# A hybrid diffusion backbone step: who adds the weight blocks of the Strassen-Winograd FFN, and when S4 is multiplied

## The chip, the cores and the metric

One Trainium2 chip, one of its cores. The metric is device time in microseconds of one execution. All arithmetic is fp32 in and out; TensorE multiplies each fp32 operand as a high part (fp32r) and a low part (the rest), three matmuls for one product.

## The reference

One layer of a transformer trunk over 128 context and 512 latent tokens (640 in all), D_MODEL = 1024, D_FF = 2816: adaLN modulation, a combined projection, two attention mixers, a gated merge, and then the FFN, the only part that the change touches:

```python
def swiglu(h, wg, wu, wd):
    return (jax.nn.silu(h @ wg) * (h @ wu)) @ wd

xs = xs + gt2 * swiglu(modulate(rmsnorm(xs, g_ffn[l]), sh2, sc2), w_gate[l], w_up[l], w_down[l])
```

The same is computed for the context tokens `xp` with their own modulation.

## The kernel before

Activations lie transposed, features on the 128 partitions and 640 tokens along a row. The FFN's 22 feature tiles are worked in three parts (`FF_PARTS = [8, 8, 6]`): in each part the gate and up tiles, then four pairs of output tiles, `w_down`, of which each part adds its share to the result in DRAM. The first three gate/up tiles are done plainly; the rest of the FFN is a list of 31 **jobs** (`JOBS`): 19 gate/up jobs (a gate tile and the up tile of one feature tile f, inner length 1024) and 12 output jobs (two output tiles; inner length 1024 in parts 0 and 1, 768 in part 2). Counting from 0, jobs 5 to 8, 17 to 20 and 27 to 30 are output jobs.

A job is a 2 x 2 block product by the Strassen-Winograd scheme: 7 products of half size in place of 8. The weights' blocks are A11, A12 (first unit of weights) and A21, A22 (second unit), each 128 x 512 elements (128 x 384 in part 2's output jobs). The 7 products have as their left sides A11, A12, A22 and four sums:

- S1 = A21 + A22, S3 = A11 + A21, S2 = A11 + S1, S4 = A12 + S2 (signs are folded into the right sides).

S1 is made in A21's place, S2 in A11's, S4 in A12's; S3 has a place of its own in `scr`. All four are made by accumulating DMAs that GpSimd (POOL) issues: S1 adds A22 from DRAM (`w_main`) onto A21 (line 657), S3 is A11 from DRAM (L660) and then A21 from DRAM added (L669), S2 adds S1's place onto A11's (L667, source in SBUF), S4 adds S2's place onto A12's (L675). S2 overwrites A11, so it waits for A11's low part; S4 waits for A12's low part and for S2. On the same queue, POOL also issues the accumulating DMAs of finished output tiles to `y_t` (L684, `add_result`), for which it waits for ScalarE's scaling (L1103).

Each left side is split before it is multiplied: ScalarE writes its high part (`left_high`, L1074), VectorE subtracts it for the low part (`left_low`, L1589). TensorE multiplies in the order of `LEFT`: A11, S1, A12, S4, S2, S3, A22, each into a PSUM bank of its own (`product`, L2071), 4 x 3 matmuls of 128 x 128 by 320 columns (3 x 3 in part 2's output jobs), so 84 (63) in a job. The results are combined by VectorE: C11 (L1598), U and V (L1602, L1604), C12 (L1606), C22 with U3 (L1611), C21 (L1618); ScalarE first copies the product P1 of A11 out of PSUM (`copy_p1`, L1082). For a gate/up job follow tanh (ScalarE, L1090), the gate product (VectorE, L1623, L1632), the high and low part of the new activation (L1043, L1535) and its own Winograd sums (L1544 to L1565), which are shorter for the first half of a part's tiles than for the second. TensorE may overwrite a bank only when it was read: A11's after P1's copy, A12's after C11, S1's and S2's after V, and so on.

The stage for weights has 4 places of one unit (`RING`), two jobs. SP loads the units (L531); a unit's place is free (`unit_used`) when the low part of S4 (first unit) or of S2 (second unit) of the job two before has been written.

The order on each engine is written out by hand in one loop over the jobs. In round j VectorE does C21 of job j-1, the low parts of S4 and S3 of job j, the activation's work, A11's low part of job j+1, C11 of j, the low parts of S1, A22, A12 of j+1, U, V, C12 of j, S2's low part of j+1, C22 of j. ScalarE's order is the same in kind, with S4's and S3's high parts at the end of the round before. POOL does, for job j+1: S1, S3's first term (after S3's low part of job j, since S3 has one place), S2, S3's second term, S4; and the results of an output job around them:

```python
            for j in range(len(JOBS)):
                more = j + 1 < len(JOBS)
                if j and JOBS[j - 1][1] is None:
                    add_result(j - 1, 1)
                if more:
                    s1_s3_first(j + 1)
                    s2_s3(j + 1)
                    s4(j + 1)
                if JOBS[j][1] is None:
                    add_result(j, 0)
```

## Time and profile before

| | us |
|---|---|
| median of 3 runs | 1013.99 (1013.25 to 1014.4) |
| the profiled execution, its own time | 1017.25 |
| its span, first to last instruction | 1015.4 |
| TensorE busy | 928.8 (91%) |
| VectorE busy | 659.0 (65%) |
| ScalarE busy | 457.9 (45%) |
| POOL busy | 151.0 (15%) |
| DMA, mean over the span | 149 GB/s |

The span is counted from the first instruction; the jobs of the FFN run from 542.9 us to 1007.6 us of it, before them come projection, attention and the plain tiles. TensorE's matmuls are pipelined and their ends are modelled, so an engine that is shown busy can still be slower than it could be; the distance from one start to the next is the measure, and so is the granted clock beside it.

### The profile page before, as it was taken

To read this page: it belongs to the slowest core of one execution; us is meant where nothing else is said; L and a number is where in the kernel's file an instruction comes from. 1 tells how busy PE (TensorE), PEld (TensorE's weight loads), DVE (VectorE), ACT (ScalarE), POOL (GpSimd) and SP (SyncE) were. 2 spreads that over 40 slices of the span, in tenths; PEclk is the share of its full clock that TensorE was granted. 3 is DMA by queue.
4 is the path that set the end of the run, shared out by engine and by line. 5 is a ranking of instruction groups with operands and counts; after the bars stand their busy time and mean duration, and the time that the engine had idled before them with its cause. 6 is when DMAs were issued, how large, how long until landed. Compare 5 with 4: busy or idle time off the path is not lost.

```text
span 1015.4 us, 16372 instructions
## 1 busy us (share of the span) xinstructions
PE 928.8 (91%) x6253; PEld 864.6 (85%) x6253; DVE 659.0 (65%) x1241; ACT 457.9 (45%) x962; POOL 151.0 (15%) x188
## 2 busy tenths in 40 slices
PE   5999999999999999999999998778899887899884
PEld 4798887788879999999999998778899887799884
DVE  4667987996886633234787886345678843578833
ACT  4653446666775222213573453333434533334432
POOL 0000000000000000000002322323223232333332
PEclk7999999999999999999999998988999999799987
DMA  9755342623442124212336778788777788877675
GB/s 374 289 190 183 115 156 78 213 70 126 136 157 62 63 84 171 79 63 63 123 128 135 173 172 173 151 155 183 154 159 180 174 181 160 156 181 182 159 148 79
DMA packets 55806, 151.66 MB, mean 149 GB/s; under 512 B 6448, under 2 KB 13744, under 8 KB 54448
## 3 DMA queue, kind: packets, MB, share of 16 engines
q1 hardware_dynamic: 31136, 100.02, 28.9%
q0 software_dynamic: 23872, 49.82, 27.7%
q8 instruction: 50, 0.82, 0.3%
q10 hardware_dynamic: 720, 0.77, 0.2%
q14 instruction: 28, 0.23, 0.1%
HBM read 122.67 MB, written 12.19 MB: 133 GB/s over the span
## 4 chain that ended last, share of the span: by engine, by line
PE 45%; DMA 26%; DVE 10%; issue 9%; ACT 4%; POOL 3%; SPq 1%; ACTq 0%; POOLq 0%; DVEq 0%
PE ps L1696 20%; DMA stage<-stage 16%; PE ps L1792 12%; DMA stage<-w_main 7%; DVE w_lo L1589 4%; PE ps L2000 3%; PE ps L1918 2%; ACT w_hi L1074 2%; PE ps L1892 2%; PE ps L1903 2%; DMA scr<-w_main 1%; POOL scr L669 1%; DVE y_lo L1535 1%; PE ps L1745 1%; ACT scr L1103 1%
## 5 line engine op out<-in xcount | busy, mean ns | idle before, releaser
L1074 ACT ACTIVATE w_hi<-stage 128x512 fp32r<-128x512 f32 (+1 forms) x186 | 107.2, 608 | 259.8 <-DMA stage<-stage 175.7
L1589 DVE TENSOR_TENSOR w_lo<-stage,w_hi 128x512 fp32r<-128x512 f32 (+1 forms) x186 | 119.6, 670 | 151.8 <-ACT w_hi L1074 151.8
L2071 PE MATMUL ps<-y_hi,w_hi 128*128 128x320 f32 x264 | 89.4, 339 | 33.0 <-DVE scr L1604 16.7
L1165 DVE TENSOR_TENSOR w_lo<-stage,w_hi 128x1024 fp32r<-128x1024 f32 x56 | 68.4, 1222 | 75.9 <-ACT w_hi L708 75.8
L2071 PE MATMUL ps<-m_hi,w_hi 128*128 128x320 f32 x304 | 97.7, 321 | 15.0 <-DVE scr L1604 15.0
L708 ACT ACTIVATE w_hi<-stage 128x1024 fp32r<-128x1024 f32 x56 | 59.1, 1061 | 91.8 <-PE ps L1696 50.9
L2071 PE MATMUL ps<-h_hi,w_hi 128*128 128x320 f32 x272 | 86.9, 320 | 13.8 <-DVE w_lo L1589 13.8
L2071 PE MATMUL ps<-m_lo,w_hi 128*128 128x320 f32 x304 | 96.9, 319 | 0.0
L2071 PE MATMUL ps<-m_hi,w_lo 128*128 128x320 f32 x304 | 96.6, 318 | 0.0
L2071 PE MATMUL ps<-y_lo,w_hi 128*128 128x320 f32 x264 | 87.6, 332 | 0.0
L2071 PE MATMUL ps<-y_hi,w_lo 128*128 128x320 f32 x264 | 87.3, 331 | 0.0
L2071 PEld LDWEIGHTS ps<-y_hi,w_hi 128*128 128x128 f32 x264 | 55.0, 208 | 37.0 <-DVE scr L1604 18.3
L2071 PE MATMUL ps<-h_lo,w_hi 128*128 128x320 f32 x272 | 85.8, 315 | 0.0
L2071 PE MATMUL ps<-h_hi,w_lo 128*128 128x320 f32 x272 | 85.8, 315 | 0.0
L1792 PE MATMUL ps<-w_hi,h_hi 128*128 128x512 f32 (+1 forms) x200 | 75.0, 375 | 0.0
L1792 PE MATMUL ps<-w_lo,h_hi 128*128 128x512 f32 (+1 forms) x200 | 73.7, 369 | 0.0
L1792 PE MATMUL ps<-w_hi,h_lo 128*128 128x512 f32 (+1 forms) x200 | 73.7, 368 | 0.0
L2071 PEld LDWEIGHTS ps<-m_hi,w_hi 128*128 128x128 f32 x304 | 59.9, 197 | 16.1 <-DVE scr L1604 16.1
L1696 PE MATMUL ps<-h_hi,w_hi 128*128 128x320 f32 x288 | 69.9, 324 | 0.7 <-ACT scr L883 0.4
L2071 PEld LDWEIGHTS ps<-h_hi,w_hi 128*128 128x128 f32 x272 | 52.7, 194 | 17.1 <-issue 17.0
L1696 PE MATMUL ps<-h_hi,w_lo 128*128 128x320 f32 x288 | 65.6, 309 | 0.0
L1696 PE MATMUL ps<-h_lo,w_hi 128*128 128x320 f32 x288 | 65.5, 309 | 0.0
(226 smaller groups left out, 2306.4 us busy)
## 6 DMA issues: line engine op xcount, KB each, us to landing
stage<-w_main SPq DMA_DIRECT2D x118, 512.0 KB, 3.7
scr<-w_main POOLq DMA_DIRECT2D x54, 256.0 KB, 4.6
stage<-stage POOLq DMA_DIRECT2D x54, 256.0 KB, 3.9
x<-w_ada SPq DMA_DIRECT2D x23, 512.0 KB, 4.5
y_t<-scr POOLq DMA_DIRECT2D x24, 320.0 KB, 4.8
qk<-w_ada SPq DMA_DIRECT2D x7, 1024.0 KB, 12.6
stage<-w_main POOLq DMA_DIRECT2D x27, 256.0 KB, 5.7
bb<-rpb SPq DMA_DIRECT2D x16, 256.0 KB, 4.0
```

The lines of the kernel that those rows point to most:

```text
L669: pool.dma_start(left_stage("S3", j), w_main[u + 1, :, 0:n], accum_op=ALU.add).then_inc(s3_sum, 16)
L708: act.activation(w_hi[:, slot, :], stage[:, slot, :], ACT.Copy).then_inc(hi_done, 1)
L1074: act.activation(w_hi[:, slot, at:at + job_half(j) * P], left_stage(op, j), ACT.Copy).then_inc(left_hi[op], 1)
L1165: dve.tensor_tensor(w_lo[:, slot, :], stage[:, slot, :], w_hi[:, slot, :].bitcast(F32), ALU.subtract).then_inc(lo_done, 1)
L1589: dve.tensor_tensor(w_lo[:, slot, w], left_stage(op, j), w_hi[:, slot, w].bitcast(F32), ALU.subtract).then_inc(left_lo[op], 1)
L1696: ins = pe.matmul(out[:, half, :], wt[:, w_slot, w], rt[:, rk, half * TH:(half + 1) * TH], start=start and n == 0, stop=stop and n == 2)
L1792: ins = pe.matmul(ps[:, acc_bank(b, i), 0:width], (h_hi, h_lo)[part][:, k, i * P:(i + 1) * P], wt[:, u % RING, at:at + width], start=k == ...
L1892: ins = pe.matmul(ps[:, hh, at:at + keys.shape[1]], qk[rows, tile, blk * P:(blk + 1) * P], keys, start=True, stop=True)
L1903: ins = pe.transpose(ps[0:n, 2 + hh, c * P:(c + 1) * P], p_sb[hh][:, at:at + n], ident)
L1918: ins = pe.matmul(ps[hh * HD:(hh + 1) * HD, 4 + p % 2, 0:P], v, pt_sb[hh][0:n, c * P:(c + 1) * P], start=c == 0, stop=c == len(parts[0]) - 1)
L2000: ins = pe.matmul(ps[:, 2 * slot + half, 0:TH], wt[:, u % RING, w], rt[:, k, half * TH:(half + 1) * TH], start=k == 0 and n == 0, stop=k = ...
L2071: ins = pe.matmul(ps[:, BANK_OF[op], 0:TH], wt[:, slot, w], right(op, part, j, k), start=k == 0 and n == 0, stop=k == half - 1 and n == 2)
```

## The change

Five edits, all in the FFN's jobs:

- **VectorE makes the four sums** of a job when the job before it is an output job (`sums_by_vector`): 11 jobs, 6, 7, 8, 9, 18, 19, 20, 21, 28, 29 and 30. The other 20 jobs keep the DMAs. Four tensor_tensor adds of 128 x 512 (128 x 384) stand in the round before that job; S3 is now A11 + A21 from the stage.
- **A11's parts of job j+1 stand ahead of S4's of job j** on VectorE and ScalarE, S4's high part moves from the end of the round before to the place behind A11's; `y_sums` moves behind them on VectorE.
- **TensorE multiplies S4 after S2**, save in the first output job of a part, where the order stays.
- **S3 has two places**, used by turns, so POOL issues S3's first term and S1 for job j+2 in round j, between S2 and S4 of job j+1.
- SP loads the second unit of a job ahead of the first; the second unit's place in job 0 is free after A22's low part.

The core of the diff:

```diff
     return sum(f is None for _, f, _ in JOBS[:j])
+def sums_by_vector(j):
+    return j > 0 and JOBS[j - 1][1] is None
+def sum_number(j):
+    return sum(sums_by_vector(i) == sums_by_vector(j) for i in range(j + 1))
+def starts_down(j):
+    return JOBS[j][1] is None and JOBS[j - 1][1] is not None
+def order_of(j):
+    return ("A11", "S1", "A12") + (("S4", "S2") if starts_down(j) else ("S2", "S4")) + ("S3", "A22")
 def jobs_before(part):
...
             if op == "S3":
-                return s3_sb[:, 0:n]
+                return (s3_sb, s3_second)[j % 2][:, 0:n]
             slot = (JOB_UNIT + 2 * j + (op in ("S1", "A22"))) % RING
...
             return slot, at + (j % 2 * 512 if op == "A22" else 0)
+        def sum_made(op, j):
+            n = sum_number(j)
+            if sums_by_vector(j):
+                return {"S1": s1_own, "S2": s2_own, "S3": s3_own, "S4": s4_own}[op], n
+            return {"S1": s1_sum, "S2": s2_sum, "S3": s3_sum, "S4": s4_sum}[op], 16 * n
         def unit_arrived(u):
...
             j, second = divmod(u - JOB_UNIT, 2)
-            return left_lo["S2" if second else "S4"], j + 1
+            return left_lo["S4" if not second else "S2" if j else "A22"], j + 1
         def slot_free(op, j):
...
             sp.dma_start(x[:, :], x_t.rearrange("p k t -> p (k t)")).then_inc(xr_in, 16)
-            for u in range(U_WO, N_UNITS):
+            for u in range(U_WO, JOB_UNIT):
                 sp.wait_ge(*unit_used(u - RING))
                 load_unit(u, u % RING)
+            for j in range(len(JOBS)):
+                for u in (JOB_UNIT + 2 * j + 1, JOB_UNIT + 2 * j):
+                    sp.wait_ge(*unit_used(u - RING))
+                    load_unit(u, u % RING)
             sp.wait_ge(out_kv, 64)
...
             pool.dma_start(y_t.rearrange("p k t -> p (k t)"), x[:, :]).then_inc(x_out, 16)
-            def s1_s3_first(j):
+            def s1(j):
                 u, n = JOB_UNIT + 2 * j, job_half(j) * P
                 pool.wait_ge(*unit_arrived(u + 1))
                 pool.dma_start(left_stage("S1", j), w_main[u + 1, :, n:2 * n], accum_op=ALU.add).then_inc(s1_sum, 16)
-                if j:
-                    pool.wait_ge(left_lo["S3"], j)
-                pool.dma_start(left_stage("S3", j), w_main[u, :, 0:n]).then_inc(s3_in, 16)
-            def s2_s3(j):
-                u, n = JOB_UNIT + 2 * j, job_half(j) * P
-                pool.wait_ge(s1_sum, 16 * (j + 1))
+            def s3_first(j):
+                if j >= 2:
+                    pool.wait_ge(left_lo["S3"], j - 1)
+                pool.dma_start(left_stage("S3", j), w_main[JOB_UNIT + 2 * j, :, 0:job_half(j) * P]).then_inc(s3_in, 16)
+            def s3_second_term(j):
+                pool.wait_ge(s3_in, 16 * sum_number(j))
+                pool.dma_start(left_stage("S3", j), w_main[JOB_UNIT + 2 * j + 1, :, 0:job_half(j) * P],
+                               accum_op=ALU.add).then_inc(s3_sum, 16)
+            def s2(j):
+                pool.wait_ge(*sum_made("S1", j))
                 pool.wait_ge(left_lo["A11"], j + 1)
                 pool.dma_start(left_stage("S2", j), left_stage("S1", j), accum_op=ALU.add).then_inc(s2_sum, 16)
-                pool.wait_ge(s3_in, 16 * (j + 1))
-                pool.dma_start(left_stage("S3", j), w_main[u + 1, :, 0:n], accum_op=ALU.add).then_inc(s3_sum, 16)
             def s4(j):
-                pool.wait_ge(s2_sum, 16 * (j + 1))
+                pool.wait_ge(*sum_made("S2", j))
                 pool.wait_ge(left_lo["A12"], j + 1)
                 pool.dma_start(left_stage("S4", j), left_stage("S2", j), accum_op=ALU.add).then_inc(s4_sum, 16)
+            def by_transfers(j):
+                return j < len(JOBS) and not sums_by_vector(j)
             def add_result(j, second):
...
                 pool.dma_start(y_t[:, n, :], kept[i], accum_op=ALU.add).then_inc(r_out[i], 16)
-            s1_s3_first(0)
-            s2_s3(0)
+            s1(0)
+            s3_first(0)
+            s2(0)
+            s3_second_term(0)
             s4(0)
+            s1(1)
+            s3_first(1)
+            s3_second_term(1)
             for j in range(len(JOBS)):
-                more = j + 1 < len(JOBS)
                 if j and JOBS[j - 1][1] is None:
                     add_result(j - 1, 1)
-                if more:
-                    s1_s3_first(j + 1)
-                    s2_s3(j + 1)
+                if by_transfers(j + 1):
+                    s2(j + 1)
+                if by_transfers(j + 2):
+                    s3_first(j + 2)
+                    s1(j + 2)
+                if by_transfers(j + 1):
                     s4(j + 1)
+                if by_transfers(j + 2):
+                    s3_second_term(j + 2)
                 if JOBS[j][1] is None:
...
             left_high("A22", 0)
-            left_high("S4", 0)
             left_high("S3", 0)
...
                     left_high("A11", j + 1)
+                left_high("S4", j)
                 copy_p1(j)
...
                 if more:
-                    left_high("S4", j + 1)
                     left_high("S3", j + 1)
...
                                   ALU.subtract).then_inc(left_lo[op], 1)
+            def s3(j):
+                dve.wait_ge(*unit_arrived(JOB_UNIT + 2 * j))
+                dve.wait_ge(*unit_arrived(JOB_UNIT + 2 * j + 1))
+                dve.wait_ge(left_lo["S3"], j - 1)
+                dve.tensor_tensor(left_stage("S3", j), left_stage("A11", j), left_stage("S1", j), ALU.add).then_inc(s3_own, 1)
+            def s1(j):
+                dve.wait_ge(*sum_made("S3", j))
+                dve.tensor_tensor(left_stage("S1", j), left_stage("S1", j), left_stage("A22", j), ALU.add).then_inc(s1_own, 1)
+            def s2(j):
+                dve.wait_ge(*sum_made("S1", j))
+                dve.wait_ge(left_lo["A11"], j + 1)
+                dve.tensor_tensor(left_stage("S2", j), left_stage("A11", j), left_stage("S1", j), ALU.add).then_inc(s2_own, 1)
+            def s4(j):
+                dve.wait_ge(*sum_made("S2", j))
+                dve.wait_ge(left_lo["A12"], j + 1)
+                dve.tensor_tensor(left_stage("S4", j), left_stage("A12", j), left_stage("S2", j), ALU.add).then_inc(s4_own, 1)
             def of_product(op):
...
                 dve.tensor_tensor(by_half[:, H_V, :], of_product("S1"), by_half[:, H_U, :], ALU.add).then_inc(v_done, 1)
+                dve.wait_ge(left_used["S4"], j + 1)
                 dve.wait_ge(v_done, j + 1)
...
                     times_up(j - 1) if j else gated_up(ended)
-                left_low("S4", j)
                 left_low("S3", j)
                 if ended is not None:
                     y_low(ended)
-                    y_sums(ended)
+                own_sums = more and sums_by_vector(j + 1)
+                if own_sums:
+                    s3(j + 1)
+                    s1(j + 1)
                 if more:
                     left_low("A11", j + 1)
+                left_low("S4", j)
+                if own_sums:
+                    s2(j + 1)
                 if ended is not None:
+                    y_sums(ended)
                     y_sums_low(ended)
                 c11(j)
                 if more:
                     left_low("S1", j + 1)
                     left_low("A22", j + 1)
                     left_low("A12", j + 1)
+                if own_sums:
+                    s4(j + 1)
                 u2_v_c12(j)
...
                                 S2=(v_done, j), S3=(c22_done, j), A22=(c21_done, j))
-                for op in LEFT:
+                for op in order_of(j):
                     pe.wait_ge(*free[op])
```

What the change moves, at the two places that the prediction speaks of. VectorE, the head of the round of gate/up job 15 (f = 15; the activation of f = 14 is worked in it), before; `hi_S4` is the semaphore of ScalarE's high part of S4, and so on:

```order
L1632 SCALAR_TENSOR_TENSOR scr<-scr 128x640 [waits c21_done,dve_own]
L1589 TENSOR_TENSOR w_lo<-stage,w_hi 128x512 [waits hi_S4]
L1589 TENSOR_TENSOR w_lo<-scr,w_hi 128x512 [waits hi_S3]
L1535 TENSOR_TENSOR y_lo<-scr,y_hi 128x640 [waits ahi_done]
L1548 TENSOR_TENSOR scr<-scr 128x640 [waits y1_lo]
L1551 TENSOR_TENSOR scr<-scr 128x320 [waits a_ready,y23_sum]
L1589 TENSOR_TENSOR w_lo<-stage,w_hi 128x512 [waits hi_A11]
L1563 TENSOR_TENSOR y_lo<-scr,y_hi 128x640 [waits y23_hi_done]
L1565 TENSOR_TENSOR h_lo<-scr,h_hi 128x320 [waits y4_hi]
L1598 TENSOR_TENSOR scr<-ps,scr 128x320 [waits p1_copied,used_A12]
```

The same round now:

```order
L1704 SCALAR_TENSOR_TENSOR scr<-scr 128x640 [waits c21_done,dve_own]
L1637 TENSOR_TENSOR w_lo<-s_second,w_hi 128x512 [waits hi_S3]
L1583 TENSOR_TENSOR y_lo<-scr,y_hi 128x640 [waits ahi_done]
L1637 TENSOR_TENSOR w_lo<-stage,w_hi 128x512 [waits hi_A11]
L1637 TENSOR_TENSOR w_lo<-stage,w_hi 128x512 [waits hi_S4]
L1596 TENSOR_TENSOR scr<-scr 128x640 [waits y1_lo]
L1599 TENSOR_TENSOR scr<-scr 128x320 [waits a_ready,y23_sum]
L1611 TENSOR_TENSOR y_lo<-scr,y_hi 128x640 [waits y23_hi_done]
L1613 TENSOR_TENSOR h_lo<-scr,h_hi 128x320 [waits y4_hi]
L1669 TENSOR_TENSOR scr<-ps,scr 128x320 [waits p1_copied,used_A12]
```

VectorE now splits A11 of the next job before S4, and S4's low part and the activation's sums follow; S3's source is the second place, since job 15 is odd.

POOL, around output jobs 6 and 7: from S4 of job 6 to S1 of job 8, before (`stage_in3` and `stage_in1` say that a second unit has arrived, `r_done` that a result is scaled):

```order
L675 DMA stage<-stage 128x512 [waits lo_A12,s2_sum]
L684 DMA y_t<-scr 128x640 [waits x_out,r_done] x2
L657 DMA stage<-w_main 128x512 [waits stage_in3]
L660 DMA scr<-w_main 128x512 [waits lo_S3]
L667 DMA stage<-stage 128x512 [waits lo_A11,s1_sum]
L669 DMA scr<-w_main 128x512 [waits s3_in]
L675 DMA stage<-stage 128x512 [waits lo_A12,s2_sum]
L684 DMA y_t<-scr 128x640 [waits x_out,r_done] x2
L657 DMA stage<-w_main 128x512 [waits stage_in1]
```

And now, from S2 and S4 of job 5, over all the output jobs of part 0, to the first transfers for job 10:

```order
L706 DMA stage<-stage 128x512 [waits lo_A11,s1_sum]
L712 DMA stage<-stage 128x512 [waits lo_A12,s2_sum]
L724 DMA y_t<-scr 128x640 [waits x_out,r_done] x4
L724 DMA y_t<-scr 128x640 [waits r_out0,x_out,r_done]
L724 DMA y_t<-scr 128x640 [waits r_out1,x_out,r_done]
L695 DMA scr<-w_main 128x512 [waits lo_S3]
L689 DMA stage<-w_main 128x512 [waits stage_in1]
L699 DMA scr<-w_main 128x512 [waits s3_in]
L724 DMA y_t<-scr 128x640 [waits r_out2,x_out,r_done]
```

Of the five sum transfers a job none is left between the results; those for job 10 stand ahead of the last results.

## Rows read from the trace of the kernel before

**Rows 1.** The page: granted clock in 40 slices of the span; the software DMA queue.

```profile
PEclk7999999999999999999999998988999999799987
...
q0 software_dynamic: 23872, 49.82, 27.7%
```

**Rows 2.** Busy time by stretch of whole jobs, L2071 (the jobs' matmuls) alone; start:end, length.

```profile
core 0: us, PE busy (x) PEld busy (x), PEclk, DMA share, GB/s
542.89:567.53 24.64, 24.64 (x168) 24.64 (x169) 1.00 0.63 160
567.53:607.06 39.53, 37.68 (x255) 36.97 (x253) 1.00 0.80 180
607.06:673.69 66.63, 56.23 (x338) 54.98 (x337) 0.90 0.80 162
673.69:710.99 37.30, 29.34 (x170) 28.58 (x169) 0.86 0.78 163
710.99:796.18 85.19, 78.28 (x506) 77.00 (x505) 0.96 0.74 167
796.18:858.34 62.16, 52.07 (x339) 50.81 (x337) 0.97 0.85 173
858.34:949.99 91.65, 79.57 (x506) 77.88 (x505) 0.94 0.75 168
949.99:1007.60 57.61, 45.13 (x254) 43.34 (x252) 0.85 0.69 129
sum 464.71, PE 402.94 PEld 394.21; mean PE 50.37 PEld 49.28
```

**Rows 3.** The chain of waits in gate/up job 14; start us, us, what.

```profile
759.03 0.64 ACT w_hi L1074
...
759.69 1.29 DVE w_lo L1589 x2
760.99 0.74 DVE y_lo L1535
...
762.98 0.61 DVE w_lo L1589
...
764.21 0.87 POOL stage L667
...
773.60 0.64 ACT w_hi L1074
```

**Rows 4.** The same view in output job 7.

```profile
649.57 0.56 POOL y_t L684
650.13 7.44 DMA stage<-w_main
...
667.54 0.56 POOL y_t L684
```

**Rows 5.** DMAs: unit loads (L531), S1's sums (L657), results (from the page's part 6).

```profile
DMA to landing us min/median/max: 3.4/3.7/17.0
...
L657 POOL DMA_DIRECT2D stage<-w_main x31: 873/1202/1224, 513.9 to 984.9; - x31
...
DMA to landing us min/median/max: 4.0/5.7/9.4
...
y_t<-scr POOLq DMA_DIRECT2D x24, 320.0 KB, 4.8
```

**Rows 6.** VectorE: a gate/up round, an output round (columns as in 2, all engines); single operations.

```profile
759.69:774.26 14.57, 12.72 (x86) 12.32 (x84) 11.97 (x20) 6.75 (x14) 4.07 (x5) 1.00 0.73 163
642.28:661.12 18.84, 14.36 (x84) 13.86 (x84) 7.59 (x14) 6.11 (x12) 5.84 (x7) 0.91 0.81 160
...
604.45 1.89 DVE L1589 TENSOR_TENSOR w_lo<-stage,w_hi 128x512 fp32r<-128x512 f32 x3
...
L1632 DVE SCALAR_TENSOR_TENSOR scr<-scr 128x640 f32<-128x640 f32 x19 | 15.7, 826 | 1.9
...
L1604 DVE TENSOR_TENSOR scr<-ps,scr 128x320 f32<-128x320 f32 x31 | 15.2, 492 | 1.1
```

6 lines of the change are left out of this document (4 added, 2 removed).

## The prediction

> **What bounds the kernel now.** I read the page's slices first: until the jobs of the FFN TensorE's granted clock is full nearly everywhere, in the last 15 slices it falls again and again [rows 1]. So the time to win lies behind 542.9 us. Next the stretches with TensorE's matmuls counted [rows 2]. In the first two jobs 168 matmuls take 24.64 us, so one takes 146.7 ns from start to start, a product of 12 takes 1.76 us and a job of 84 takes 12.32 us. That pace is the floor: the 31 jobs hold 27 x 84 + 4 x 63 = 2520 matmuls, 369.6 us, and they take 464.7 us. The excess is **95.1 us**. Stretch by stretch (length minus matmuls x 146.7 ns, counting whole jobs): jobs 2 to 4 have 2.6 us over the floor, the output jobs 5 to 8 17.4, jobs 9 and 10 12.7, gate/up jobs 11 to 16 11.3, output jobs 17 to 20 12.9, jobs 21 to 26 17.7, the short output jobs 27 to 30 20.7 (four times 9.24 us from 57.61). TensorE is shown busy for 402.9 us, so 61.8 us of the excess are idle and 33.3 us are matmuls that ran slowly; the granted clock averages 0.85 to 0.97 in all stretches from job 5 on, a mixture of the levels 1.2 and 2.4 GHz, and 1.00 in the first five jobs, where the waits are short [rows 2]. What goes from the waits takes this along.
>
> Then the chain of waits, for what ends them. In a gate/up job [rows 3] it is a ring that comes back after 14.57 us (759.03 to 773.60): S4's sum has landed, ScalarE makes its high part, VectorE its low part and S3's, then the activation's low part and its sums, and only then A11's low part of the next job (ends 763.59). That one frees POOL to issue S2 in A11's place, behind it S3's second term, and S4 on top of S2: 10.0 us from A11's low part until S4 has landed and ScalarE takes it up. TensorE needs S4 fourth. In an output job [rows 4] the ring is longer: POOL issues S1 only behind the second result's transfer, S1 takes 7.44 us (up to 9.4 over all, [rows 5]) beside that result and two units, then come S1's, A22's and A12's parts, S4's sum, ScalarE's scaling, the next result. The ring takes 18 us (649.57 to 667.54).
>
> **Gate/up jobs.** Now A11's low part waits for C21, the gate product, S3's low part and the activation's low part, not for S4. By the durations of [rows 3, 6] this is 0.16 + 0.50 + 0.83 + 0.61 + 0.74 + 0.61 = 3.5 us after the job's start. S4 of the next job lands 10.0 us later, at 13.5 us. TensorE wants it at 12.32 + 4 x 1.76 = 19.36 us, since it is now the fifth product; less 0.64 us for the high part and 0.65 us for the low part, it may land until 18.0 us. A slack of 4.5 us stands where TensorE waited. S1 and S3's terms are issued one job earlier, beside S2, and wanted after more than 12 us. The unit loads keep theirs: the first unit starts when S4's low part ends, at 4.1 us, takes 3.7 us [rows 5] and is wanted at 14.8 us. What S4's wait would hold on ScalarE's queue is P1's copy, on VectorE's everything up to V, wanted at 14.1 us; at a landing of 13.5 us, 1.2 us after the next job's start, nothing is held.
>
> What is late next? VectorE: the dearest round (activation of the second half of a part) keeps it busy 11.97 us [rows 6], of 12.32. It fits, and what it lags by is covered by the 3 us between S4's low part and its product. I leave 0.3 us a job for 15 gate/up jobs by transfers (the first two of the 17 show none now): **4.5 us**, between 0, as in jobs 0 and 1, and 1.9, as in jobs 11 to 16 today (11.3 / 6) [rows 2]; nearer to 0 because of the slack.
>
> **Output jobs, and the job behind them.** For 11 jobs five transfers go from POOL's queue. Software transfers take 27.7% of 1015.4 us for 49.82 MB [rows 1], so 1.48 us of all 16 DMA engines for 0.262 MB and 7.4 us for five. The DMA engines are busy 0.80 x 66.63 / 4 = 13.3 us per output job today [rows 2], over the floor of 12.32 even if nothing waited; 5.9 us remain. POOL's queue then holds results alone, and S1's wait for a result is gone. Against this stand four adds on VectorE. No such add is in the trace; the nearest row, the low part, has the same sizes and two inputs in SBUF, and three in a row take 1.89 us [rows 6], 0.61 us each behind another. I take 4 x 0.61 = 2.4 us (bounds 0.49 each as for 320 columns, L1604, and 0.83 each as for 640, L1632: 2.0 and 3.3 us). An output round has 7.59 us of VectorE now [rows 6], so 10.0 us, under 12.32. In order: C21 at 0.7 us, S3's low part 1.3, adds S3 and S1 2.6, A11 3.2, S4 low 3.8 (wanted at 7.0), add S2 4.4; C11, three low parts, add S4 by 8.5; U, V, C12 by 10.1. Each has over a microsecond to spare. The short jobs: 9.24 us against some 8.8 of VectorE, tight but under. I leave 0.25 us for each of the 11: **2.8 us** (0 to 1.9 each, as above).
>
> The Trainium skill has a formula for this add (VectorE: DVE Perf Modes, the section on the TRN2 errata for SBUF sources): an fp32 tensor_tensor takes (N + 151)/0.96 ns, 691 ns for 512. By it three in a row would take 2.07 us, and the trace shows 1.89. By the page the adds cost 2.8 us a round in place of 2.4; the measured distance decides.
>
> The **first output job** of a part is the hard one. Its round has the dear activation work without one gate product and with four adds: 11.97 - 0.82 + 2.44 = 13.6 us, over 12.32. And S4 stays fourth there, wanted at 5.28 us, with its low part at 3.5 + 1.2 (adds S3, S1) + 0.6 = 5.4 us plus VectorE's lag of about 0.5 us. So 0.7 to 1 us each in parts 0 and 1; in part 2 S4 is wanted at 3.96 us, so 1.5 us. S2 needs the last activation's sums, at 8.9 us for its last quarter, just in time. **3.5 us** for the three, between 0 and the 17.4/4 = 4.4 us each that they and their followers have today.
>
> **Edits at nothing.** The PSUM banks: C12 now waits for S4's product, which ends at 8.96 us, before VectorE comes to it at 10.1. S3's second place costs memory alone. SP's new order of units delays a first unit by one load, 3.7 us, under a slack of 6 us. Before 542.9 us POOL's S1 of job 0 comes one load later; it was issued at 513.9 us [rows 5], 29 us before TensorE needs it. The last result after the last matmul (1007.6 us to the end, 7.8 us) stays.
>
> **Sum.** 95.1 - (4.5 + 2.8 + 3.5) = 84.3 us less. The profiled span of 1015.4 us becomes 931; its own time, 1017.25 us, lies 3 us over the median of the runs, and the difference taken from the median, 1013.99, gives **930 us**. Case A, chance 0.72, from 920 (no waits left, 1014 - 95 = 919) to 940.
>
> **Rival 1: the transfers set the pace of the gate/up jobs.** They need 0.74 x 85.19 / 6 = 10.5 us of the DMA engines per job [rows 2], which at 12.32 us is a share of 0.85. For: the shares seen over whole stretches are 0.63 to 0.85, and the first unit's load now starts with S2 instead of 3 us before it. Against: the floor pace of jobs 0 and 1 and the share of 0.85 in jobs 17 to 20. If they fill no more than 0.80, a job takes 13.1 us, 17 x 0.8 = 13.6 us more: 944 us. Chance 0.12. The Trainium skill (DMA: Bandwidth & Descriptors, Issuing engines are not separate DMA queues) says that transfers of all queues interleave on the same 16 engines; by that rule S2 would land later by the load beside it. No row here separates the two.
>
> **Rival 2: VectorE becomes the bound.** If its instructions cost 0.08 us more than their distance in a row shows (0.83 us for one of 640 columns alone, L1632 [rows 6], 0.74 us of distance for the activation's low part [rows 3]), 17 of them make the dearest rounds 13.3 us: 8 x 1.0 + 3 x 1.6 = 13 us more, 943 us. For: 11.97 of 12.32 us. Against: that the busy time was counted with the real distances. Chance 0.06.
>
> **Rival 3: the adds don't free the output jobs**, another wait takes their place, such as the result's slot or the activation's. If half of the 63.7 us over the floor in jobs 5 to 10, 17 to 20 and 27 to 30 stays, in place of about 6: 956 us. Against: a result lands in 4.8 us even in today's traffic [rows 5], and its slot is wanted two jobs later. Chance 0.05.
>
> **Rival 4, slower than before: the loads hold VectorE.** In output jobs there is a new ring of one job: first unit lands, adds S3 and S1, A11's and S4's low parts (2.5 us), and S4's low part starts the next first unit's load. It is L + 2.5 us for a landing time L. At 3.7 us that is 6.2. It binds above L = 9.8, and is worse than today's 16.1 us (66.63 + 62.16, by 8) above 13.6. The longest landing in the trace is 17.0 us [rows 5]: then 19.5 us a job, 6 x 3.4 + 2 x 0.9 + 3 x 5.1 = 37 us more than today (jobs 9 and 10 take 18.65 us each, the short ones 14.4), against 27 us won in the gate/up jobs: 1024 us. That landing is one of 118, the median is 3.7 [rows 5], and the new output jobs have less traffic. Chance 0.04.
>
> **How the numbers follow.** 930 us is case A. The range of 920 to 950 takes in A and rivals 1 and 2, 0.90 of the chance less a tail of A's; it leaves out rivals 3 and 4 and what I have not thought of (0.01). A difference under 0.2% (2 us) can't be told from none: faster 0.95, same 0.01, slower 0.04.
>
> **What would show it.** TensorE's start-to-start distance of jobs at 12.3 us from one end of the FFN to the other, with 1 us more in jobs 5, 17 and 27; the granted clock at 1.00 there; the chain of waits through TensorE and no longer through the sums; the DMA share near 0.85 in gate/up jobs and near 0.5 in output jobs; VectorE's idle time before S4's low part small. I am wrong if the gate/up jobs take 13 us at a DMA share of 0.8 (rival 1), if VectorE never idles there (rival 2), if output jobs show a wait for a result or a unit (rivals 3, 4).

## The result, and the profile after

| | before | after |
|---|---|---|
| median of 4 runs each, us | 1014.12 (1013.25 to 1014.4) | 932.18 (929.59 to 933.48) |
| ratio of after to before, 95% interval | | 0.919 (0.9169 to 0.9211) |
| span of the profiled execution | 1015.4 | 927.7 |
| the 31 jobs, first matmul to the end of the last | 464.7 | 378.7 |
| of it over the floor of 369.6 | 95.1 | 9.1 |

The change takes off 81.9 us; the forecast was a time of 930 us, so 84 us. The part before the jobs differs by several microseconds from run to run (they begin between 541.3 and 546.3 us in the kernels below), so small differences are read from the length of the jobs' stretch, and not from the whole time alone.

The page of the kernel after, as in [rows 1] and [rows 5]: granted clock and DMA share in 40 slices, the software queue, results.

```profile
PEclk8999999999999999999999999999999999999999
DMA  9854433542454122422205289747999856889746
...
q0 software_dynamic: 16704, 36.38, 22.2%
...
y_t<-scr POOLq DMA_DIRECT2D x24, 320.0 KB, 5.6
```

The clock is at 0.9 or more in each of the last 15 slices. Windows of the kernel after by the same stretches as [rows 2], its product line alone:

```profile
core 0: us, PE busy (x) PEld busy (x), PEclk, DMA share, GB/s
541.91:566.55 24.64, 24.64 (x168) 24.64 (x169) 1.00 0.84 189
566.55:603.51 36.96, 36.96 (x254) 36.96 (x253) 1.00 0.81 173
603.51:654.69 51.18, 49.51 (x338) 49.28 (x337) 1.00 0.64 141
654.69:679.33 24.64, 24.64 (x170) 24.64 (x169) 1.00 0.92 199
679.33:753.25 73.92, 73.92 (x506) 73.92 (x505) 1.00 0.87 186
753.25:805.55 52.30, 49.77 (x338) 49.28 (x337) 1.00 0.63 135
805.55:879.47 73.92, 73.92 (x506) 73.92 (x505) 1.00 0.86 187
879.47:920.60 41.13, 39.38 (x254) 38.39 (x252) 0.96 0.56 104
sum 378.69, PE 372.74 PEld 371.03; mean PE 46.59 PEld 46.38
```

All 19 gate/up jobs take 12.32 us, the floor. TensorE's idle time in the jobs fell from 61.8 to 5.9 us (378.69 - 372.74), and what its matmuls took over the floor from 33.3 to 3.1 us (372.74 - 369.6): the clock did come back with the waits. The 9.1 us that are left lie in the output stretches: 1.90 us in job 5, 3.02 in job 17, 3.66 in job 27 and 0.5 us in jobs 29 and 30. The waits of TensorE in the jobs (line, what ended them: us in all, times, longest) are five:

```profile
PE ps L2151 <- issue: 4.9, 3, 1.9
PE ps L2151 <- DVE y_lo L1583: 0.9, 2, 0.7
```

The three of "issue" stand ahead of S4's product in jobs 5, 17 and 27. The two others are in jobs 17 and 27, ahead of the last three matmuls of A12's product, which need the low part of the last activation; VectorE makes it late for the same reason. Here is job 17, VectorE's timeline in its first eight microseconds (start, us, line); job 17 starts at 753.25:

```profile
755.80 0.48 DVE L1690 TENSOR_TENSOR scr<-ps,scr 128x320 f32<-128x320 f32 x1
...
757.14 0.69 DVE L1637 TENSOR_TENSOR w_lo<-s_second,w_hi 128x512 fp32r<-128x512 f32 x1
758.03 0.83 DVE L1583 TENSOR_TENSOR y_lo<-scr,y_hi 128x640 fp32r<-128x640 f32 x1 [0.20 <-ACT y_hi L1092]
758.77 0.68 DVE L1644 TENSOR_TENSOR scr<-stage 128x512 f32<-128x512 f32 x1
759.49 0.69 DVE L1649 TENSOR_TENSOR stage<-stage 128x512 f32<-128x512 f32 x1
760.10 1.28 DVE L1637 TENSOR_TENSOR w_lo<-stage,w_hi 128x512 fp32r<-128x512 f32 x2
```

C21 of the job before (L1690) starts 2.55 us after job 17 has begun. S4's low part is the second of the pair at 760.10 and ends at 761.38; S4's product starts 0.10 us behind it, so the wait that the view calls "issue" is one for VectorE. TensorE's timeline:

```profile
761.48 0.38 PE L2151 MATMUL ps<-y_hi,w_hi 128*128 128x320 f32 x1 [1.88 <-issue]
```

Where does that lateness come from? VectorE's timeline in the rounds before job 5: the two waits that a round with the activation of the second half of a part has (a dear round), and C21's starts on both sides of one such round:

```profile
581.72 0.83 DVE L1583 TENSOR_TENSOR y_lo<-scr,y_hi 128x640 fp32r<-128x640 f32 x1 [0.20 <-ACT y_hi L1092]
585.28 0.83 DVE L1611 TENSOR_TENSOR y_lo<-scr,y_hi 128x640 fp32r<-128x640 f32 x1 [0.28 <-ACT y_hi L1105]
592.22 0.49 DVE L1690 TENSOR_TENSOR scr<-ps,scr 128x320 f32<-128x320 f32 x1
...
604.95 0.49 DVE L1690 TENSOR_TENSOR scr<-ps,scr 128x320 f32<-128x320 f32 x1
```

The dear round takes VectorE **12.73 us** (592.22 to 604.95), not less than 12.32. So VectorE falls behind TensorE by 0.41 us in each, hidden by S4's slack until S4 is wanted fourth. By C21, job 5 meets a lag of 1.3 us, job 17 one of 2.4 us (C21 would be due 0.16 us after the start), job 27 one of 0.7 us.

Three dear rounds make 1.2 us, so they explain job 5 and only half of job 17. The other half comes in a single round, that of job 14: C21 starts at 716.50 and then at 730.34, 13.84 us later; the two rounds behind it take 12.73 us each. In it ScalarE's high part and then VectorE's low part of S2 wait for S2's transfer, ScalarE's and VectorE's timelines:

```profile
727.60 0.63 ACT L1123 ACTIVATE w_hi<-stage 128x512 fp32r<-128x512 f32 x1 [3.05 <-DMA stage<-stage]
728.26 0.69 DVE L1637 TENSOR_TENSOR w_lo<-stage,w_hi 128x512 fp32r<-128x512 f32 x1 [1.01 <-ACT w_hi L1123]
...
730.34 0.48 DVE L1690 TENSOR_TENSOR scr<-ps,scr 128x320 f32<-128x320 f32 x1
```

That transfer, issued at 720.88, took 6.7 us. In jobs 9 and 21 S2 took 7.0 and 7.5 us, and VectorE entered the next job 1.3 and 1.8 us behind; there light rounds followed, which take 11.8 to 12.3 us, and the lag was gone by job 14 and down to 0.6 us by job 25.

In the short job 27 the clock makes the delay longer: behind the wait of 1.34 us ahead of S4's product it falls. Windows of S4's and S2's product in job 27, the product line alone:

```profile
885.48:889.73 4.25, 4.24 (x19) 4.25 (x19) 0.60 0.41 123
```

Two products of 1.32 us at full clock take 4.25 us there, at a mean of 0.60, a mixture of the levels 1.2 and 2.4 GHz: 1.6 of job 27's 3.66 us.

POOL's timeline in a gate/up stretch shows the transfers of one round (L706 is S2, L695 S3's first term, L689 S1, L712 S4):

```profile
720.88 0.86 POOL L706 DMA_DIRECT2D stage<-stage  x1 [5.20 <-DVE w_lo L1637]
721.43 0.89 POOL L695 DMA_DIRECT2D scr<-w_main  x1
721.99 1.22 POOL L689 DMA_DIRECT2D stage<-w_main  x1
728.02 0.88 POOL L712 DMA_DIRECT2D stage<-stage  x1 [4.81 <-DMA stage<-stage]
```

S4 is issued 7.1 us after S2 in this round, and 5.3 to 5.9 us in most others; before the change it was 3.4 to 5.6 us. S2's landing went from 3.0/3.4/5.3 us before (minimum, median, maximum, 31 of them) to

```profile
DMA to landing us min/median/max: 3.4/5.3/7.5
```

in 20: S2 now has a unit's load, S3's first term and S1 beside it. The Trainium skill (DMA: Bandwidth & Descriptors, Issuing engines are not separate DMA queues) says that DMAs of all engines run on the same 16 DMA engines and interleave. The longer landing, 5.3 in place of 3.4 us, agrees with that. In these rounds S4 lands 13.5 to 16.3 us after the start of the job in which it is issued, where 13.5 had been forecast and 18.0 was, by the prediction's count, the latest that costs nothing. So S4's slack took it; what it did not take is VectorE's wait for S2 itself, above.

### The profile page after: what moved, and what is told of

Its sections match the earlier page's. It is cut to its first block and busy times, and to the rows that moved or that the text cites. A ratio compares the mean times of both kernels' runs of the same rounds, so it can differ in the third digit from the quotient of the medians.

```text
span 927.7 us, 16403 instructions
## 1 busy us (share of the span) xinstructions
PE 897.1 (97%) x6253; PEld 840.1 (91%) x6253; DVE 684.5 (74%) x1285; ACT 460.4 (50%) x962; POOL 105.6 (11%) x133
## 5 line engine op out<-in xcount | busy, mean ns | idle before, releaser
L1637 DVE TENSOR_TENSOR w_lo<-stage,w_hi 128x512 fp32r<-128x512 f32 (+1 forms) x186 | 116.8, 669 | 21.7 <-ACT w_hi L1123 21.1
L2151 PE MATMUL ps<-m_hi,w_hi 128*128 128x320 f32 x304 | 93.9, 309 | 0.0
L2151 PE MATMUL ps<-m_lo,w_hi 128*128 128x320 f32 x304 | 93.9, 309 | 0.0
L2151 PE MATMUL ps<-y_hi,w_hi 128*128 128x320 f32 x264 | 82.8, 314 | 5.9 <-issue 4.9
L2151 PE MATMUL ps<-h_hi,w_hi 128*128 128x320 f32 x272 | 84.0, 309 | 0.0
L2151 PE MATMUL ps<-y_hi,w_lo 128*128 128x320 f32 x264 | 82.2, 311 | 0.0
L2151 PE MATMUL ps<-y_lo,w_hi 128*128 128x320 f32 x264 | 82.2, 311 | 0.0
L1776 PE MATMUL ps<-h_hi,w_hi 128*128 128x320 f32 x288 | 69.9, 324 | 0.7 <-ACT scr L932 0.4
L943 ACT ACTIVATE scr<-scr,small 128x385 f32<-128x385 f32 (+5 forms) x80 | 46.3, 582 | 27.6 <-DVE small L1401 27.3
L2151 PEld LDWEIGHTS ps<-m_lo,w_hi 128*128 128x128 f32 x304 | 57.1, 188 | 0.0
L2151 PEld LDWEIGHTS ps<-m_hi,w_lo 128*128 128x128 f32 x304 | 57.1, 188 | 0.0
```

The costliest lines, as they stand in the source:

```text
L943: act.activation(e_sb[hh][:, lo:end], s_neg[hh][:, lo:end], ACT.Exp, bias=nmax[:, r % 4:r % 4 + 1], scale=-1.0, accum_out=rsum[:, r % 4:r ...
L1637: dve.tensor_tensor(w_lo[:, slot, w], left_stage(op, j), w_hi[:, slot, w].bitcast(F32), ALU.subtract).then_inc(left_lo[op], 1)
L1776: ins = pe.matmul(out[:, half, :], wt[:, w_slot, w], rt[:, rk, half * TH:(half + 1) * TH], start=start and n == 0, stop=stop and n == 2)
L2151: ins = pe.matmul(ps[:, BANK_OF[op], 0:TH], wt[:, slot, w], right(op, part, j, k), start=k == 0 and n == 0, stop=k == half - 1 and n == 2)
```

## The experiments

Each kernel was timed beside the kernel before on the same chip; the three batches' medians of it are 1014.43 (e1 to e4), 1015.93 (e5, e7, e8, e9) and 1013.57 us (e6, e12 to e14). The ratio is to that. "Stretch" is the length of the 31 jobs (before 464.7, after 378.7 us).

| kernel | median us | ratio (95%) | stretch us |
|---|---|---|---|
| e1 no adds by VectorE | 948.98 | 0.937 (0.9335 to 0.9404) | 394.7 |
| e2 kernel before, with the adds | 958.89 | 0.9467 (0.9437 to 0.9498) | 403.8 |
| e3 S4 fourth everywhere | 936.37 | 0.9244 (0.9212 to 0.9275) | 383.6 |
| e4 S4's parts ahead of A11's | 935.33 | 0.9249 (0.9211 to 0.9286) | 382.2 |
| e5 both orders back | 936.86 | 0.9255 (0.9204 to 0.9305) | 380.4 |
| e6 nearly all sums by VectorE | 965.03 | 0.9527 (0.9487 to 0.9568) | 413.4 |
| e7 adds late in the first output job | 929.49 | 0.9174 (0.913 to 0.9218) | 378.3 |
| e8 POOL's order as before | 945.13 | 0.9327 (0.9275 to 0.938) | 393.9 |
| e9 transfers for the second output job | 925.65 | 0.9133 (0.9092 to 0.9173) | 373.9 |
| e12 the same, and A11 ahead of the activation | 922.34 | 0.9103 (0.907 to 0.9136) | 370.4 |
| e13 POOL's order and the adds only | 959.46 | 0.9472 (0.9432 to 0.9513) | 406.4 |
| e14 POOL's order only | 991.58 | 0.9783 (0.9743 to 0.9823) | 436.0 |

### What the adds are worth: e1, e2 and e6

e1 is the kernel after with every sum by a transfer:

```diff
 def sums_by_vector(j):
-    return j > 0 and JOBS[j - 1][1] is None
+    return False
```

> The changed kernel with all sums by transfers again (the new orders, S4 after S2 and two places for S3 stay). My theory (two separate gains: the orders free the gate/up jobs, VectorE's adds free the output jobs, which are limited by their transfers): gate/up jobs stay at 12.32 us; output jobs need 13.3 us of all DMA engines each and take 14.5 to 15.5 us, short ones 11 to 11.5; in all 950 to 962 us. Rival (the output jobs were held by the order on POOL's queue alone, S1 behind the results, and not by the transfers' amount): they fall to 12.3 us too, 932 to 936 us. Second rival (without the adds everything falls back): about 1010 us.

It takes 948.98 us, 1 us below the range; the stretch is 16.0 us longer than with the adds. The loss lies at the end of each group of output jobs, and not where the output jobs begin (without the adds jobs 17 and 27 are even 2.3 and 2.4 us shorter): windows of e1 for jobs 5 to 7, 8 to 10, and 11 to 16:

```profile
603.79:642.57 38.78, 37.45 (x254) 36.96 (x253) 1.00 0.96 207
642.57:686.57 44.00, 39.08 (x255) 38.38 (x253) 0.96 0.95 205
686.57:760.49 73.92, 73.92 (x507) 73.92 (x505) 1.00 0.90 193
```

Jobs 6 and 7 run at 12.32 us even with five transfers each, where 14.5 to 15.5 us had been expected. Jobs 8 to 10 take 13.21, 14.32 and 16.46 us, while ScalarE waits for S2's sum:

```profile
ACT w_hi L1123 <- DMA stage<-stage: 24.0, 4, 7.5
```

This is the wait that the adds take away. What makes S2 late is told by ScalarE's and POOL's timelines in jobs 8 and 9 (ACT: S2's high parts; L724: the second result of job 7; L706: S2 of job 9):

```profile
644.65 0.63 ACT L1123 ACTIVATE w_hi<-stage 128x512 fp32r<-128x512 f32 x1 [6.90 <-DMA stage<-stage]
...
649.21 0.88 POOL L724 DMA_DIRECT2D y_t<-scr  x1 [1.52 <-ACT scr L1152]
653.05 0.86 POOL L706 DMA_DIRECT2D stage<-stage  x1 [2.96 <-issue]
...
658.96 0.63 ACT L1123 ACTIVATE w_hi<-stage 128x512 fp32r<-128x512 f32 x1 [7.51 <-DMA stage<-stage]
```

It is a ring again, of 14.31 us: S2's parts, C21 and the scaling behind them, the result's transfer, and S2 of the next job behind that in POOL's queue. A11's low part, which S2 also waits for, was ready at 649.6; S2 is issued 3.4 us later, 2.96 of them idle time for which the profile shows no cause, with the DMA engines 0.95 busy. Whether full DMA engines or the order in POOL's queue cost the 16 us is not separated.

e2 is the kernel before with the four adds alone, put into VectorE's and POOL's orders of that time:

```diff
-                if more:
+                if more and not sums_by_vector(j + 1):
                     s1_s3_first(j + 1)
...
+                own_sums = more and sums_by_vector(j + 1)
+                if own_sums:
+                    s3(j + 1)
+                    s1(j + 1)
                 if more:
                     left_low("A11", j + 1)
+                if own_sums:
+                    s2(j + 1)
...
+                if own_sums:
+                    s4(j + 1)
                 u2_v_c12(j)
```

> The kernel before with nothing but the adds on VectorE for the 11 jobs. My theory: jobs 6 to 9, 18 to 21 and 28 to 30 go to 12.3 us (short ones 9.3), the other gate/up jobs keep the ring through S4 and take 13 to 16 us as before, the first output jobs keep their 3 to 6.5 us: 48 us of the 95 remain, about 967 us (960 to 975). Rival (the adds lengthen VectorE's queue so that output jobs gain little): 985 to 1000 us.

958.89 us, 1 us below the range: two thirds of the change's gain from this part alone. Jobs 6 to 9, 18 to 21 and 28 to 30 stand at the floor, as in the kernel after; gate/up jobs 10 to 16 take 13.0 to 15.9 us, with the ring of [rows 3] still in them (14.81 us from S4's high part of job 14 to that of job 15).

e6 asks for the other side, adds in all jobs from 2 on:

```diff
 def sums_by_vector(j):
-    return j > 0 and JOBS[j - 1][1] is None
+    return j > 1
```

> The changed kernel with the sums of all jobs from 2 on by VectorE: no sum by transfers is left but those of jobs 0 and 1. My theory (VectorE's dear rounds take 12.73 us now and four adds cost 2.44): dear rounds of 15.2 us, the others of 13 us, TensorE waits for VectorE: 8 x 2.9 + 8 x 0.6 = 28 us more, 950 to 962 us, VectorE never idle in gate/up jobs. Rival (the DMA share of 0.87 costs as much as the adds): 932 us or less.

965.03 us, a little over the range given. The window of job 15, all engines, in the columns of the round in [rows 6]:

```profile
744.78:761.77 16.99, 14.28 (x87) 13.86 (x85) 15.95 (x28) 6.63 (x13) 0.00 (x0) 0.90 0.20 62
```

VectorE is busy 15.95 of 16.99 us of job 15 with the DMA engines at 0.20: here VectorE is the bound, in the dear rounds (jobs 14 to 16 take 15.0 us on average, 15.2 had been expected). The light rounds in front of them stay at 12.3 to 13.5 us. So the four adds pay where the round has room for them, which is behind an output job.

### What the orders are worth: e3, e4 and e5

```diff
 def order_of(j):
-    return ("A11", "S1", "A12") + (("S4", "S2") if starts_down(j) else ("S2", "S4")) + ("S3", "A22")
+    return ("A11", "S1", "A12") + ("S4", "S2") + ("S3", "A22")
```

> The changed kernel with TensorE's old order in every job (S4 fourth, wanted 1.76 us earlier). My theory: S4's low part is ready 4.1 us plus VectorE's lag after a job's start, wanted at 5.28 us; the lag is over 1.2 us only in jobs 15 to 17 and 26, 27: 2 to 5 us more, 934 to 938 us. Rival (the place of S4's product is what frees the gate/up jobs): 1 to 2 us in each of 17 gate/up jobs, 950 to 965 us.

936.37 us, as expected: 4.9 us more in the stretch. Jobs 1 to 4, 6, 16, 18, 22 and 28 are 0.4 to 1.8 us longer than in the kernel after, in waits for S4's low part; jobs 17 and 27 are 1.3 us shorter, since VectorE comes to them 1.1 and 0.3 us behind and not 2.4 and 0.7. VectorE's lag now meets a product that is wanted 1.76 us earlier. Jobs 1 to 4 hold 3.2 of the 4.9 us, and VectorE was 1.7 us behind at job 1 in this execution, 0.15 us in that of the kernel after. It was 1.5 and 2.0 us behind in e7 and e9 too, whose edits don't touch these jobs, so part of the 4.9 us may be a difference between executions.

e4 puts S4's parts back ahead of A11's on both engines and leaves the rest (`y_sums`, VectorE's two adds for the activation's Winograd sums, stays behind A11's low part):

```diff
-                left_high("S4", j)
                 copy_p1(j)
...
                 if more:
+                    left_high("S4", j + 1)
                     left_high("S3", j + 1)
...
+                left_low("S4", j)
                 left_low("S3", j)
...
                 if more:
                     left_low("A11", j + 1)
-                left_low("S4", j)
```

> The changed kernel with S4's high and low parts back ahead of A11's (TensorE's and POOL's orders, the adds and y_sums stay as changed). My theory: the ring is back, S4 landed, its parts, S3's, the activation's low part, A11's low part: 3.3 us, and 10 to 11 us until the next S4 has landed, so 13.3 to 14.3 us a job for the 15 gate/up jobs by transfers behind another such: 15 to 30 us more, 947 to 962 us. Rival (this order is immaterial, S4's later product and POOL's order do it): 931 to 935 us.

**A miss**: 935.33 us, 3.5 us in the stretch where at least 15 had been expected. The gate/up jobs but one stay at 12.32 us; jobs 17, 26 and 27 are 0.8 to 2.2 us longer than in the kernel after, job 5 is 0.8 us shorter. S4's low part holds A11's again, so the ring is back, but it is a shorter one: POOL's timeline of e4,

```profile
725.35 0.86 POOL L706 DMA_DIRECT2D stage<-stage  x1 [6.80 <-DVE w_lo L1638]
...
730.31 0.88 POOL L712 DMA_DIRECT2D stage<-stage  x1 [2.64 <-DVE w_lo L1638]
...
737.88 0.85 POOL L706 DMA_DIRECT2D stage<-stage  x1 [5.60 <-DVE w_lo L1638]
```

S2 comes back after 12.53 us, where the ring before took 14.57 [rows 3]. S4 no longer waits for S3's second term on POOL, and `y_sums` is no longer inside. The 12.53 us are still over 12.32, but such rounds come only three in a row, and VectorE's lag (4.2 us at job 17) is what shows of them.

e5 takes both orders back together:

> The two runs before in one: S4's parts ahead of A11's and S4 multiplied fourth in every job; the adds, POOL's order, S3's two places and y_sums behind A11 stay. My theory now (the ring through S4 is 12.6 us long without S3's second term in it, 0.3 us over TensorE's 12.32, and was hidden by the 1.76 us that the fifth place gives): now it shows, 0.3 us in each of 15 gate/up jobs and 0.5 us to get there in each part, on top of what both did alone: 940 to 946 us. Rival (the two edits are worth their single prices and no more, 4 and 3 us): 937 to 940 us. Second rival (each covers for the other fully, the old ring of 14.5 us is back): 955 to 970 us.

936.86 us, the stretch 1.7 us longer than after, below what was expected and at the lower edge of the rival's range: the rival was right in kind. Jobs 6 to 16 and 18 to 24 stand at 12.32 us. Differences of 2 to 3 us between these three runs are too near to the noise to be told apart. **With `y_sums` behind A11's low part and POOL's new order, the order of S4 against A11 and against S2, the edits that the prediction gave the gate/up jobs' gain to, are worth 2 to 5 us of the 82, together or apart.** All three runs keep `y_sums` where the change put it. The kernel after with `y_sums` alone put back was not run, so it is not shown whether the opened ring would have freed the gate/up jobs without that move.

### What then won the gate/up jobs: e8, e13 and e14

e8 is the kernel after with POOL's order of before and one place for S3:

```diff
-                return (s3_sb, s3_second)[j % 2][:, 0:n]
+                return s3_sb[:, 0:n]
...
                 if by_transfers(j + 1):
+                    s1(j + 1)
+                    s3_first(j + 1)
                     s2(j + 1)
-                if by_transfers(j + 2):
-                    s3_first(j + 2)
-                    s1(j + 2)
-                if by_transfers(j + 1):
+                    s3_second_term(j + 1)
                     s4(j + 1)
-                if by_transfers(j + 2):
-                    s3_second_term(j + 2)
```

> The changed kernel with POOL's old order for the jobs by transfers (S1, S3's first term, S2, S3's second term, S4 of job j+1, all in round j) and one place for S3. Theory A (the slack of 4.5 us at S4 covers the second term in front of it, so POOL's order is not needed): 931 to 937 us. Theory B (S4 lands 1 us later and S3 later than ScalarE asks for it at the end of the round, which holds ScalarE's and VectorE's queues): gate/up jobs of 12.8 to 13.5 us, 940 to 955 us.

945.13 us, as theory B had it; 15.2 us more in the stretch, in the dear rounds and the jobs behind them (job 5 18.61, job 15 13.39, job 17 17.30 us) and in jobs 10 and 22, the first by transfers behind a group of output jobs (14.06 and 14.10 us). S1's and S3's transfers a job ahead, with the second place that they need, carry this; S3's second place alone was not tried.

e13 is e5 with one more edit, `y_sums` back ahead of A11's low part; what it keeps of the change is POOL's order with S3's two places, SP's order and the adds:

```diff
                 if ended is not None:
                     y_low(ended)
+                    y_sums(ended)
...
                 if ended is not None:
-                    y_sums(ended)
                     y_sums_low(ended)
```

> The kernel before with the adds on VectorE, POOL's new order, S3's two places and SP's order of units; TensorE's, VectorE's and ScalarE's orders all as before, y_sums too. Theory A (POOL's order frees the gate/up jobs, the engines' orders are worth only some 5 us in the first output jobs): 937 to 941 us. Theory B (moving y_sums behind A11's low part, 1.3 us out of the ring, did it): the ring is 12.6 + 1.3 = 13.9 us in dear rounds and 13.0 in the others, 950 to 958 us.

959.46 us, a little over theory B's range, against e5's 936.86: this one edit, two adds of VectorE moved behind one other instruction, is worth 22 us with the orders as in e5 (the stretch 406.4 against 380.4). Windows of jobs 11 to 16, first in e5, then in e13:

```profile
682.35:756.27 73.92, 73.92 (x507) 73.92 (x505) 1.00 0.85 184
```

```profile
686.03:773.04 87.01, 76.58 (x506) 75.18 (x505) 0.98 0.71 158
```

The chain of waits of e13 in jobs 14 and 15 is the ring of [rows 3] again, now with the two sums (L1597, L1600) between the activation's low part and A11's:

```profile
733.23 0.64 ACT w_hi L1123
...
733.89 1.29 DVE w_lo L1638 x2
735.19 0.73 DVE y_lo L1584
735.92 0.75 DVE scr L1597
...
736.69 0.49 DVE scr L1600
737.18 0.61 DVE w_lo L1638
...
738.51 3.37 DMA stage<-stage
...
742.32 6.78 DMA stage<-stage
...
749.12 0.64 ACT w_hi L1123
```

It comes back after 15.9 us. The sums' own part of it is 1.26 us. What is longer besides is S4's transfer, 6.8 us: it is issued 3.8 us after S2, while S3's first term and S1 (issued at 739.06 and 739.62) still run; in e5 S4 is issued 5.0 us after S2, when A12's low part allows it, and ScalarE has it some 4.4 us later. How much of the 22 us belongs to the 1.26 us and how much to that collision isn't separated.

e14 is e13 without the adds, so the kernel before with POOL's and SP's order of the change and S3's two places:

```diff
 def sums_by_vector(j):
-    return j > 0 and JOBS[j - 1][1] is None
+    return False
```

> The same without the adds: POOL's new order, S3's two places and SP's order are all that is left of the change. If the adds and POOL's order are the two gains: 17 us more than the run before it, as between the changed kernel and the one with all sums by transfers, 953 to 960 us. If the adds are needed for POOL's order to help: 980 us or more.

991.58 us, 22 us less than before, and in the range of the second case: the adds are needed for POOL's order to help as it does in the change. With the adds (e13) it is 959.5, no better than the adds without POOL's order (e2, 958.9). **The parts don't add up.** The adds take 55 us off the kernel before (e2), 32 off e14 and 17 in the kernel after; POOL's order takes 22 off before, nothing on top of the adds, and 13 in the kernel after (e8). The readings above fit one picture, which is argued and not tried by itself: a job's pace is set by the longest of several rings (through S4, and in output jobs through the result and S2) and the floor, so a part that shortens one of them is worth little while another is longer, and little more once all are near 12.32 us. `y_sums` moved alone in the kernel before was not tried.

### What is left, the first output job: e7, e9 and e12

e7 moves adds S3, S1 and S2 of the first output job's round behind `y_sums_low`, out of the way of S4's low part:

```diff
-                if own_sums:
+                if own_sums and not starts_down(j):
                     s3(j + 1)
                     s1(j + 1)
...
                     y_sums_low(ended)
+                if own_sums and starts_down(j):
+                    s3(j + 1)
+                    s1(j + 1)
+                    s2(j + 1)
```

> The changed kernel with VectorE's adds S3, S1 and S2 behind the activation's sums in the first output job of a part (jobs 5, 17, 27) alone. My theory (the 8.6 us left over the floor there are S4's low part behind two adds on VectorE, 1.3 us, and VectorE's lag): 1.3 to 1.8 us less in each of the three, 3.5 to 5 us in all, 927 to 929 us. Rival (what is left is the activation's chain alone, the adds lie beside it): no change, 932 us.

929.49 us, and 0.4 us less in the stretch than after, no more than noise, where 3.5 to 5 us had been expected: job 17 goes from 15.34 to 14.13 and job 27 from 12.90 to 10.57 us, but jobs 6, 18 and 28 rise to 12.69, 12.69 and 11.31 us. The work was moved, not removed, and the debt is paid a job later. Job 5 takes 14.32 us, no less than after: VectorE came to it 2.7 us behind in this execution, against 1.3.

e9 removes it: the job behind the first output job has its sums by transfers again, in the one round that has room on POOL and none on VectorE.

```diff
 def sums_by_vector(j):
-    return j > 0 and JOBS[j - 1][1] is None
+    return j > 1 and JOBS[j - 1][1] is None and JOBS[j - 2][1] is None
```

> The changed kernel with the sums of jobs 6, 18 and 28 by transfers again, so VectorE has no adds in the rounds of jobs 5, 17 and 27. My theory: as with the adds late, S4's low part comes 1.3 us earlier, and VectorE's round is 2.4 us shorter, which nothing asks for: 927 to 929 us. Rival (the transfers land late behind those of job 5 and the results): 932 to 938 us.

925.65 us, 4.8 us less in the stretch, a little better than expected. Jobs 17 and 27 take 13.83 and 9.94 us, but job 5 still takes 14.27: the lag of the dear rounds is untouched, and in this execution VectorE was 2.0 us behind at job 1 already and 2.65 us at job 5.

e12 goes at that lag: on top of e9, in every round that works an activation, save the first output job's, A11's parts stand ahead of the activation's high and low part, and C11 ahead of `y_sums_low`, so that VectorE has work while ScalarE makes the high parts. Since A11's low part is earlier, so is S2's transfer (4.10 us after job 14's start, 4.59 in the kernel after).

```diff
                 left_low("S3", j)
...
+                first = ended is not None and not starts_down(j)
+                if first:
+                    left_low("A11", j + 1)
                 if ended is not None:
                     y_low(ended)
...
+                if first:
+                    c11(j)
+                if ended is not None:
                     y_sums_low(ended)
```

(e7's edit is in its source too, but with e9's condition no round has both.)

> The run with transfers for jobs 6, 18 and 28, and in the rounds of gate/up jobs A11's parts ahead of the activation's high and low parts, and C11 ahead of the low parts of the activation's sums, so that VectorE has other work while it waits 0.2 and 0.28 us for ScalarE. My theory (what is left in jobs 5, 17 and 27 is VectorE's lag, 0.41 us a dear round, since such a round takes 12.73 us): the round falls to about 12.3 us, the lag of up to 1.3 us a part goes, 2 to 3 us less than with the transfers alone, 922 to 924 us. Rival (the lag comes from elsewhere, from a wait for a sum): no change, 925 to 926 us.

922.34 us, as expected, and the best of all: 0.9103 of the time before, an interval (0.907 to 0.9136) that lies below the change's (0.9169 to 0.9211). The stretch is 370.4 us, 0.8 over the floor; job 5 takes 12.38, job 17 12.32 and job 27 9.79 us. VectorE's dear rounds take 12.0 to 12.4 us from C21 to C21, that of job 14 with the wait for S2 among them. TensorE's only wait in the jobs:

```profile
PE ps L2165 <- issue: 0.2, 1, 0.2
```

## Why the prediction was right, point by point

- **The floor and where the time was to win** held: every matmul of the jobs is at 146.7 ns but for some in the three first output jobs and one in job 29, and what the clock cost (33.3 us) went with the waits. The sum said that 10.8 of the 95.1 us would stay, and 9.1 did. The stretch fell by 86.0 us, against 84.3 forecast, and 1.7 us went outside it. The medians fell by 81.9, since the profiled execution before lay 3.1 us above its median and that after 2.6 below.
- **That the sum came out this near is partly luck.** The allowances were 6.8 us too large and the first output jobs 5.1 us too small, and the two errors cancel; the next two points take them one by one.
- **The two allowances** of 0.3 us for 15 gate/up jobs and 0.25 us for 11 others, 7.3 us, were too much: all of it is 0.5 us. The slack left nothing to allow for, though it was 1.7 to 4.5 us and not 4.5 throughout. The four adds take about what was said: 0.60 to 0.72 us each from its start to the next, 2.5 us for the four, against 2.4.
- **The first output jobs** were under-sized: 3.5 us was given, 8.6 us are there. The step that failed is "plus VectorE's lag of about 0.5 us". From [rows 6] the dear round had 11.97 us busy of 12.32 and was held to fit. But busy time leaves out the waits inside the round: it takes 12.73 us from C21 to C21, 0.48 of them waits for ScalarE's high parts, and three such rounds give a lag of 1.2 us. At job 17 the lag is 2.4 us, since VectorE also waited 1.01 us for S2's parts in job 14, a wait that no step had. In job 17 S4's low part ended 8.1 us after the start, in job 5 7.0, not 5.9. That the clock would fall behind such a wait (1.6 us in job 27) was in no step either. e9, which takes the adds from that round, and e12, which on top of it fills those waits, bring the stretch 8.3 us down: VectorE's lag is the cause, tried. How it divides between the waits for ScalarE and the one for S2 is read from the trace alone, since e12 also issues S2 earlier.
- **The mechanism of the gate/up jobs was half right.** The ring was read rightly, and its members in the forecast's chain are the ones that e13 shows. But the prediction had "Now A11's low part waits for C21, ... not for S4" carry the gain. e4 and e5 show the ring closed again with the jobs at 12.32 us, but for jobs 25 and 26. So opening it was not needed once it was short; whether it would have been enough without `y_sums`' move isn't shown. What made it short: `y_sums` out of it (e13 against e5) and S1's and S3's transfers a job ahead (e8), of which the prediction had the first as an item of the ring before and the second in a clause, both without a price of their own. What the opened ring gives, in company with these, is slack that only job 26 and the first output jobs use.
- **S2's landing**: "S4 of the next job lands 10.0 us later" left out the company that S2 gets. S4 landed up to 16.3 us after the job's start, not at 13.5. For S4 the slack covered it; for S2's own low part, which stands in VectorE's queue ahead of C22, C21 and all that follows, there was no such slack, and about half of the lag at job 17 comes from it.
- **Rival 1** (the DMA engines fill no more than 0.80): refuted at 0.92 in jobs 9 and 10, with TensorE never idle. If there is such a limit it lies higher: e1 ran jobs 5 to 7 at 0.96, and lost time at 0.95 in jobs 8 to 10 with the order in POOL's queue as another possible cause.
- **Rival 2** (VectorE the bound): not at 943 us, but its mechanism is the one that bounds what is left, and e6 shows it in full.
- **Rival 3** (another wait takes the place in the output jobs): none does; jobs 6 to 8 and 18 to 20 take 12.32 us. e2 shows the adds alone do this.
- **Rival 4** (the loads hold VectorE): nearly nothing. One add of 44 waits for a unit: at 904.92, in job 29, for 1.27 us, when a load issued at 896.96 behind S4's low part took 7.94 us to land. It is the forecast's ring of L + 2.5 us in one place, and job 29 takes 9.58 us instead of 9.24. The unit loads' median landing is 3.9 us.
